# Another order of the query blocks in a differential attention loop on one core

## The chip, the cores and the metric

The kernel runs on one core of one Trainium2 chip, as one program. The metric is the device time of one launch in microseconds (us). Five engines work side by side, each through its own list of instructions in order, and they wait for each other with semaphores: TensorE (PE, matmuls and transposes), VectorE (DVE), ScalarE (ACT), GpSimd (POOL) and SyncE (SP), which starts the transfers.

## What is computed

Two blocks one after the other, on 512 latent tokens of width 1024: two layers with neighbourhood attention, differential attention and a convolution, the first of which also updates 256 context tokens, and then six further sublayers (feed-forward, recurrences, stick-breaking attention). The change lies in the differential attention of layer 0:

```python
def _diff_attend(q1, q2, k1, k2, v, lam):
    '''(softmax(q1 k1^T) - lam * softmax(q2 k2^T)) v, swept over 128-query blocks.'''
    def blk(qs):
        a, b = qs
        s1 = jnp.einsum('bqhd,bkhd->bhqk', a, k1).astype(jnp.float32) * scale
        s2 = jnp.einsum('bqhd,bkhd->bhqk', b, k2).astype(jnp.float32) * scale
        w = jax.nn.softmax(s1, axis=-1) - lam * jax.nn.softmax(s2, axis=-1)
        return jnp.einsum('bhqk,bkhe->bqhe', w.astype(v.dtype), v)
...
b_out = _diff_merge(_diff_attend(rope(q[..., :d]), rope(q[..., d:]), k1, k2, vd, lam), ...)
if update_ctx:      # layer 0 only
    b_c = _diff_merge(_diff_attend(qc[..., :d], qc[..., d:], kc[..., :d], kc[..., d:], vc, lam), ...)
```

There are four heads. The 512 latent queries attend to 768 keys (512 latent and 256 context), the 256 context queries to the 256 context keys alone. The result of each block is normalised over its 96 values and multiplied with a gate.

## The kernel before

Everything runs in fp32 (weights are split into two rounded parts for PE). A stage is a Python object with one method for each engine (`pe`, `act`, `dve`, `pool`) that writes this engine's instructions in order; nothing reorders them afterwards. `LateStage` is the second half of a layer: projections, convolution, and then the differential attention as a loop that is spread over PE, ACT and DVE. POOL has no part in it.

The loop runs over `self.steps` (L1415), a list of pairs (head, query block). In layer 0 `total` is `TA` = 768 tokens, so a head has six blocks of 128 queries: blocks 0 to 3 are latent, 4 and 5 are context. `keys` (L1549) gives 768 keys for blocks 0 to 3, called long or L here, and 256 for 4 and 5, short or S. The list has 24 entries, numbered through as "block 0" to "block 23" below (entry k, whatever its place in the head). In layer 1 `total` is 512, and all 16 entries are long.

What one entry k goes through, with the lines of the profile:

- PE, `scores_pe` (L1601): the scores of both softmaxes, six matmuls of 256 keys (two if short). It waits for the exponentials of entry k-2, whose banks it takes.
- DVE, `max_dve` (L1778): one maximum over both score rows (2 x 768 or 2 x 256).
- ACT, `exp_act` (L1708): two exponentials with sums, waiting for the maximum.
- DVE, `combine_dve` (L1786, L1788, L1791): reciprocals of the sums, and one instruction that joins both into the weights.
- PE, `turn_pe` (L354 by the helper): six transposes, or two if short. It waits for the joined weights, for L1772 of entry k-2 and for ACT's copy of entry k-1; the last four also for L1760 of entry k-1.
- ACT, `copy_act` (L1695, L1699): the transposed weights from PSUM, 256 columns, and 512 more if long.
- PE, `values_pe`: six matmuls with the values, or two.
- DVE, `o_dve` (L1760): scales the output. ACT, `root_act` (L1684, L1686, L1688): its inverse root mean square. DVE, `norm_dve` (L1766): multiplies by it.
- PE, `back_pe`: one transpose back. DVE, `fin_dve` (L1772): multiplies the gate with it.

These steps are skewed by a fixed pattern. In turn k of its loop (L1582) PE does values(k-3), back(k-4), turn(k-2), scores(k+1). ACT (L1672) does root(k-3), copy(k-2), exp(k). DVE (L1743) does:

```python
o_dve(k - 3); fin_dve(k - 4); max_dve(k); combine_dve(k - 1); norm_dve(k - 3)
```

At the end of the loop `drain` puts the begin of the output projection between the last entries: ACT and POOL or DVE split its input pieces (L897, L906), and PE runs three steps of it in each of turns 25 and 26.

PE's matmuls are all recorded on L345 and its transposes on L354, since a helper writes them; an fp32 matmul has two records, a transpose has one.

Of the kernel before, what the change touches and what calls it, by code (L numbers as in the profile page):

```python
# [18 lines left out]
P = 128  # L19
# [4 lines left out]
TA = T + TC  # L24
# [5 lines left out]
DF_HEADS, DF_QK = 4, 48  # L30
# [160 lines left out]
def build(nc, ins, out_dram):  # L191
# [6 lines left out]
    with ctx:  # L198
# [31 lines left out]
        class Area:  # L230
            made = 0

            def __init__(self, start=None):
                self.at = work_at if start is None else start
                self.end = (h_at + 4 * 2 * DT * TA) if start is not None and start < work_at else work_at + 4 * WORK
# [1156 lines left out]
        class LateStage:  # L1392
            def __init__(self, l, total, place, mix, norm, mod):
                self.l, self.total, self.mix, self.tag, self.mod = l, total, mix, f"late{l}", mod
                self.kd, self.qd = place.take(4, TA), place.take(4, TA)
                self.v_at = place.at
                self.v = place.take(6, NA_W)
                self.conv_at = place.at
                self.u = place.take(2, CONV_TOK)
                self.raw = [place.take(T) for _ in range(2)]  # L1400
                self.tmp = [place.take(T) for _ in range(2)]
                self.y = place.take(2, CONV_OUT)
                self.ln_sq = [place.take(T) for _ in range(2)]
                names = lambda g: [(f"w_in{l}", i) for i in IN_PIECE[g]]
                self.conv_of = [Project(names(8), P, norm, total), Project(names(9), P, norm, total)]
                self.k_of = Project(names(2), P, norm, TA)
                self.v_of = ToTokens(Project(names(3), P, norm, TA), self.v, self.raw)
                self.q_of = Project(names(6), P, norm, total)
                self.g_of = Project(names(7), DF_V, norm, total)
                place = Area(h_at)  # L1410
                self.p1, self.p2 = [place.take(TA) for _ in range(2)], [place.take(TA) for _ in range(2)]
                self.pt = [place.take(TA) for _ in range(2)]
                self.o_sb, self.o_sq = [place.take(DF_V) for _ in range(2)], place.take(DF_V)
                self.h_end = place.at
                self.steps = [(h_, i) for h_ in range(DF_HEADS) for i in range(total // P)]  # L1415
                self.n = len(self.steps)
                two = total == TA

                self.taps_at = (10, 6, 4, 2, 4) if two else (10, 6, 4, 4, 2)

                self.ln_at = {"mean": 1, "square": (1, 3), "sum": (2, 4), "root": (2, 4), "silu": 6} if two else {
                    "mean": 0, "square": (0,), "sum": (1,), "root": (1,), "silu": 2}
                self.starts = {0: PAD, T: PAD + T + PAD}
                self.n_y = T if total == T else CONV_OUT
# [2052 lines left out]
```

## Time and profile before

| | |
|---|---|
| time, median of 3 runs | 3408.81 us (3407.46 to 3411.09) |
| the profiled execution | 3408.95 us, of which the span 3407.20 us |
| PE busy in the span | 3203.2 us, 94% |
| DVE, ACT, POOL busy | 1675.6, 1212.0, 715.3 us |
| loop of layer 0, first to last L1760 | 468.64 to 563.30 us from the span's start |
| loop of layer 1, the same | 977.57 to 1045.82 us |

The profile is of one execution. Its times count from the begin of the span. Busy time of PE is modelled at the ends of matmuls, so a PE that reads as busy is not at its peak. A timeline row gives the start, the time taken, the engine, the line, the operation, what it writes and reads, how many instructions are merged in it, and in brackets how long the engine idled before it and which engine and line it had waited for.

### The profile page before, as it was taken

How to read it: one execution, taken by the hardware profiler on the slowest of the kernel's cores; microseconds unless marked ns; L12 is line 12 of the kernel's file. 1: busy time of each engine (PE TensorE's matmuls, PEld its weight loads, DVE VectorE, ACT ScalarE, POOL GpSimd, SP SyncE). 2: the span in 40 equal slices, each digit the busy share in tenths (PEclk: the TensorE clock that was granted, in tenths of full speed). 3: DMA queues.
4: the chain of work that ended last, by engine and by line, in shares of the span. 5: the costliest groups of instructions: out<-in, count | busy, mean ns of one | idle time of the engine just before them, and what ended most of it. 6: DMA issues, size and time to landing. Idle time of an engine off the chain costs nothing.

```text
span 3407.2 us, 40024 instructions
## 1 busy us (share of the span) xinstructions
PE 3203.2 (94%) x16252; PEld 2527.6 (74%) x16252; DVE 1675.6 (49%) x2558; ACT 1212.0 (36%) x2068; POOL 715.3 (21%) x518
## 2 busy tenths in 40 slices
PE   6999988899988999989899999999999999999998
PEld 4777766677866788867788778887888776578886
DVE  2155555415764634457655553446444525564344
ACT  3242165434264322233344332224222325542222
POOL 3204312331513100046332300001000343230000
PEclk9999999999999999999899999999999999999999
DMA  5303210121102233222000133222232231022322
GB/s 225 118 20 115 88 41 24 49 97 47 56 28 78 81 93 105 88 89 93 19 7 1 50 103 108 93 93 87 87 105 87 81 111 38 1 87 93 107 86 80
DMA packets 77575, 260.55 MB, mean 76 GB/s; under 512 B 8400, under 2 KB 9552, under 8 KB 76240
## 3 DMA queue, kind: packets, MB, share of 16 engines
q1 hardware_dynamic: 76528, 253.28, 22.6%
q0 software_dynamic: 864, 4.72, 0.4%
q8 instruction: 129, 2.11, 0.3%
q14 instruction: 54, 0.44, 0.0%
HBM read 255.87 MB, written 2.10 MB: 76 GB/s over the span
## 4 chain that ended last, share of the span: by engine, by line
PE 86%; DVE 7%; ACT 4%; POOL 1%; issue 1%; DMA 1%; SPq 0%; ACTq 0%; DVEq 0%; POOLq 0%
PE banks L345 85%; PE banks L354 1%; POOL w_lo L336 1%; DVE area L576 1%; DVE x_lat L579 1%; DMA area<-in_w_mod 1%; DVE small L1778 0%; DVE area L1722 0%; DVE area L1760 0%; ACT area L434 0%; POOL w_late L336 0%; ACT area L437 0%; ACT w_hi L326 0%; POOL area L410 0%; DVE area L494 0%
## 5 line engine op out<-in xcount | busy, mean ns | idle before, releaser
L345 PE MATMUL banks<-area,w_hi 128*128 128x512 f32 (+4 forms) x5896 | 1770.5, 383 | 24.0 <-POOL w_lo L336 8.1
L345 PEld LDWEIGHTS banks<-area,w_hi 128*128 128x128 f32 (+2 forms) x5896 | 1078.8, 188 | 288.4 <-issue 24.2
L345 PE MATMUL banks<-area,w_lo 128*128 128x512 f32 (+4 forms) x2948 | 1120.2, 381 | 0.0
L345 PEld LDWEIGHTS banks<-area,w_lo 128*128 128x128 f32 (+2 forms) x2948 | 554.8, 188 | 119.1
L345 PE MATMUL banks<-area,w_late 128*128 128x512 f32 (+2 forms) x2316 | 579.1, 399 | 28.8 <-ACT area L532 14.8
L326 ACT ACTIVATE w_hi<-w_raw 128x1024 fp32r<-128x1024 f32 (+2 forms) x361 | 349.5, 971 | 544.9 <-PE banks L345 413.4
L345 PEld LDWEIGHTS banks<-area,w_late 128*128 128x128 f32 (+1 forms) x2316 | 434.6, 190 | 146.3 <-ACT area L532 18.1
L345 PE MATMUL banks<-area,area 128*128 128x64 f32 (+10 forms) x3896 | 468.6, 326 | 71.7 <-DMA area<-in_w_mod 17.5
L345 PEld LDWEIGHTS banks<-area,area 128*128 128x128 f32 (+4 forms) x3896 | 384.0, 183 | 157.7 <-issue 71.9
L410 POOL TENSOR_TENSOR area<-area,area 128x512 f32<-128x512 f32 (+1 forms) x102 | 139.6, 1371 | 1475.2 <-ACT area L395 1473.4
L336 POOL TENSOR_TENSOR w_lo<-w_raw,w_hi 128x1024 fp32r<-128x1024 f32 (+1 forms) x133 | 308.7, 2323 | 455.4 <-ACT w_hi L326 455.4
L336 DVE TENSOR_TENSOR w_lo<-w_raw,w_hi 128x1024 fp32r<-128x1024 f32 (+1 forms) x228 | 263.2, 1155 | 158.7 <-ACT w_hi L326 158.7
L969 ACT ACTIVATE area<-area 128x512 fp32r<-128x512 f32 x88 | 55.6, 632 | 417.7 <-DVE area L1000 417.7
L326 ACT ACTIVATE w_late<-w_raw 128x1024 fp32r<-128x1024 f32 (+2 forms) x103 | 100.9, 979 | 235.9 <-PE banks L345 232.8
L345 PE MATMUL banks<-area,const 128*128 128x512 f32 (+4 forms) x422 | 149.2, 500 | 28.4 <-POOL area L410 8.2
L997 DVE TENSOR_TENSOR area<-banks,area 128x512 f32<-128x512 f32 x80 | 55.2, 691 | 239.1 <-PE banks L345 239.1
L1722 DVE SCALAR_TENSOR_TENSOR area<-area,par,area 128x783 f32<-128x783 f32 (+1 forms) x120 | 149.1, 1302 | 0.0
L862 DVE COPY area<-banks 128x512 f32<-128x512 f32 x72 | 46.9, 661 | 195.4 <-PE banks L345 179.1
L345 PEld LDWEIGHTS banks<-area,const 128*128 128x128 f32 (+3 forms) x422 | 69.4, 193 | 80.5 <-issue 33.7
L336 DVE TENSOR_TENSOR w_late<-w_raw,w_late 128x1024 fp32r<-128x1024 f32 (+1 forms) x76 | 86.1, 1133 | 85.4 <-ACT w_late L326 85.4
L989 DVE TENSOR_TENSOR area<-banks,area 128x512 f32<-128x512 f32 x80 | 55.3, 691 | 105.0 <-PE banks L345 105.0
L354 PE MATMUL banks<-const,area 128*128 128x128 f32 (+1 forms) x438 | 72.3, 284 | 33.9 <-DVE area L1772 21.4
(236 smaller groups left out, 2274.6 us busy)
## 6 DMA issues: line engine op xcount, KB each, us to landing
w_raw<-in_l_ffn_w_in SPq DMA_DIRECT2D x176, 512.0 KB, 3.2
w_raw<-in_l_ffn_w_out SPq DMA_DIRECT2D x128, 384.0 KB, 3.1
w_raw<-in_w_in SPq DMA_DIRECT2D x66, 512.0 KB, 3.5
w_raw<-in_w_mod SPq DMA_DIRECT2D x32, 512.0 KB, 5.4
w_raw<-in_w_qkv SPq DMA_DIRECT2D x24, 512.0 KB, 3.2
w_raw<-in_l_w_in SPq DMA_DIRECT2D x22, 512.0 KB, 3.3
w_raw<-in_w_out SPq DMA_DIRECT2D x32, 320.0 KB, 2.9
area<-in_w_mod SPq DMA_DIRECT2D x8, 1024.0 KB, 16.6
```

The lines of the kernel that those rows point to most:

```text
L326: e.activation(split_bufs(m)[0], raw_of(m), ACT.Copy).then_inc(*sig("w_rounded", "weights hi", m))
L336: e.tensor_tensor(lo, raw_of(m), hi.bitcast(f32), SUB).then_inc(*sig("w_split_dve" if dve else "w_split", "weights", m))
L345: return e.matmul(out, lhsT, rhs, start=first, stop=stop, skip_group_check=True)
L354: return e.transpose(out, in_, ident[0:k, 0:k])
L410: e.tensor_tensor(a, a, self.slot_of(s, j)[:, 0:c1 - c0], ADD).then_inc(*sig("squares_added", *self.tag, "added", s, j))
L576: e.scalar_tensor_tensor(y, y, self.gain(j, s), self.squares.rs[:, c0:c1], MUL, MUL).then_inc(*sig("post_step", self.tag, "step", s, j))
L579: e.tensor_tensor(x, x, y, ADD).then_inc(*sig("x_new", self.tag, "x", s, j))
L862: e.tensor_copy(yy, b).then_inc(*sig("evicted_dve", "evicted", u))
L969: e.activation(self.a_hi[:, j, :], a, ACT.Copy).then_inc(*sig("a_hi", self.tag, "a hi", half, j))
L989: e.tensor_tensor(sg, bank, self.norm.rs, MUL).then_inc(*sig("evicted_dve", "evicted", u))
L997: e.tensor_tensor(a, bank, self.norm.rs, MUL).then_inc(*sig("evicted_dve", "evicted", u))
L1722: e.scalar_tensor_tensor(yy, uu, w, yy, MUL, ADD).then_inc(*sig("taps", self.tag, "tap", m, k))
```

## The change

Within each head of layer 0 the six query blocks are taken in the order 0, 1, 4, 2, 3, 5. The two short blocks, the fourth and fifth index, are apart by two long ones now. Layer 1 keeps its order.

```diff
-                self.steps = [(h_, i) for h_ in range(DF_HEADS) for i in range(total // P)]
+                blocks = (0, 1, 4, 2, 3, 5) if total == TA else range(total // P)
+                self.steps = [(h_, i) for h_ in range(DF_HEADS) for i in blocks]
```

All engines take their order from this list, and buffers go by the entry's number, so waits and buffers stay as they were. The last entry of a head is short in both. Lines below L1415 move down by one.

On PE, in turns 4 to 7 of the loop, the rows before are (`const` is the identity, area_95 and area_96 the joined weights, area_84 and area_85 queries and keys, area_86 the values, area_99 and area_100 the transposed weights, area_101 and area_102 the outputs):

```order
L354 MATMUL banks<-const,area_95 128x128 x6
L345 MATMUL banks<-area_84,area_85 128x256 x2
L345 MATMUL banks<-area_86,area_99 128x96 x6
L354 MATMUL banks<-const,area_102 96x128
L354 MATMUL banks<-const,area_96 128x128 x6
L345 MATMUL banks<-area_84,area_85 128x256 x6
L345 MATMUL banks<-area_86,area_100 128x96 x6
L354 MATMUL banks<-const,area_101 96x128
L354 MATMUL banks<-const,area_95 128x128 x2
L345 MATMUL banks<-area_84,area_85 128x256 x6
L345 MATMUL banks<-area_86,area_99 128x96 x2
```

and now:

```order
L354 MATMUL banks<-const,area_95 128x128 x2
L345 MATMUL banks<-area_84,area_85 128x256 x2
L345 MATMUL banks<-area_86,area_99 128x96 x2
L354 MATMUL banks<-const,area_102 96x128
L354 MATMUL banks<-const,area_96 128x128 x6
L345 MATMUL banks<-area_84,area_85 128x256 x6
L345 MATMUL banks<-area_86,area_100 128x96 x6
L354 MATMUL banks<-const,area_101 96x128
L354 MATMUL banks<-const,area_95 128x128 x6
L345 MATMUL banks<-area_84,area_85 128x256 x6
L345 MATMUL banks<-area_86,area_99 128x96 x6
```

Before, the scores of entry 5 (x2) stand between long transposes and long values, and entry 4 has short transposes and values around long scores. Now entry 2's transposes and values and entry 5's scores are all short and stand together, and everything from entry 3 to entry 4 is long.

On ACT, turn 4 of the loop before (root of entry 1, copies of entry 2, exponentials of entry 4):

```order
L1684 ACTIVATE area_103,small<-area_102 128x96
L1686 ACTIVATE small<-small,const 128x1
L1688 ACTIVATE small<-small 128x1
L1695 ACTIVATE area_99<-banks 128x256
L1699 ACTIVATE area_99<-banks 128x512
L1708 ACTIVATE area_95,small<-banks,small 128x256
L1708 ACTIVATE area_97,small<-banks,small 128x256
```

and now:

```order
L1685 ACTIVATE area_103,small<-area_102 128x96
L1687 ACTIVATE small<-small,const 128x1
L1689 ACTIVATE small<-small 128x1
L1696 ACTIVATE area_99<-banks 128x256
L1709 ACTIVATE area_95,small<-banks,small 128x768
L1709 ACTIVATE area_97,small<-banks,small 128x768
```

The copy of entry 2 lost its second part, and the exponentials of entry 4 are long.

On PE, at the end of the loop, before:

```order
L354 MATMUL banks<-const,area_96 128x128 x6
L345 MATMUL banks<-area_86,area_100 128x96 x6
L354 MATMUL banks<-const,area_101 96x128
L354 MATMUL banks<-const,area_95 128x128 x2
L345 MATMUL banks<-area_86,area_99 128x96 x2
L354 MATMUL banks<-const,area_102 96x128
```

and now:

```order
L354 MATMUL banks<-const,area_96 128x128 x6
L345 MATMUL banks<-area_86,area_100 128x96 x6
L354 MATMUL banks<-const,area_101 96x128
L354 MATMUL banks<-const,area_95 128x128 x6
L345 MATMUL banks<-area_86,area_99 128x96 x6
L354 MATMUL banks<-const,area_102 96x128
```

Entry 22 is now long (x6), where before both last entries were short.

## Rows read from the trace of the kernel before

**Rows 1.** The page, part 1: busy us (share of the span) xinstructions.
```profile
PE 3203.2 (94%) x16252; PEld 2527.6 (74%) x16252; DVE 1675.6 (49%) x2558; ACT 1212.0 (36%) x2068; POOL 715.3 (21%) x518
```

**Rows 2.** Windows: stretch, its length, busy us of each engine, PEclk the granted clock.
```profile
457.70:465.10 7.40, 3.69 (x16) 2.70 (x17) 5.53 (x7) 3.74 (x9) 0.00 (x0) 0.55 0.08 32
465.10:557.40 92.30, 73.88 (x538) 55.77 (x536) 71.89 (x158) 71.61 (x219) 2.72 (x2) 1.00 0.00 1
554.00:557.40 3.40, 1.42 (x8) 0.84 (x7) 3.33 (x8) 3.08 (x8) 2.65 (x2) 1.00 0.00 0
557.40:560.80 3.40, 2.85 (x10) 2.49 (x11) 1.78 (x4) 2.72 (x7) 2.49 (x2) 0.50 0.00 0
```

**Rows 3.** Timeline, DVE, loop of layer 0, L1760: start, us, instruction, [idle before].
```profile
468.64 0.32 DVE L1760 TENSOR_SCALAR area<-banks,small 128x96 f32<-128x96 f32 x1 [1.12 <-PE banks L345]
...
492.99 0.32 DVE L1760 TENSOR_SCALAR area<-banks,small 128x96 f32<-128x96 f32 x1 [0.81 <-PE banks L345]
...
496.92 0.32 DVE L1760 TENSOR_SCALAR area<-banks,small 128x96 f32<-128x96 f32 x1
...
500.91 0.32 DVE L1760 TENSOR_SCALAR area<-banks,small 128x96 f32<-128x96 f32 x1 [1.20 <-PE banks L345]
...
505.51 0.32 DVE L1760 TENSOR_SCALAR area<-banks,small 128x96 f32<-128x96 f32 x1 [2.41 <-PE banks L345]
...
508.79 0.32 DVE L1760 TENSOR_SCALAR area<-banks,small 128x96 f32<-128x96 f32 x1
...
512.67 0.31 DVE L1760 TENSOR_SCALAR area<-banks,small 128x96 f32<-128x96 f32 x1
...
517.55 0.32 DVE L1760 TENSOR_SCALAR area<-banks,small 128x96 f32<-128x96 f32 x1 [0.81 <-PE banks L345]
...
553.94 0.32 DVE L1760 TENSOR_SCALAR area<-banks,small 128x96 f32<-128x96 f32 x1 [1.74 <-PE banks L345]
...
557.24 0.31 DVE L1760 TENSOR_SCALAR area<-banks,small 128x96 f32<-128x96 f32 x1
...
563.30 0.32 DVE L1760 TENSOR_SCALAR area<-banks,small 128x96 f32<-128x96 f32 x1 [3.37 <-PE banks L345]
```

**Rows 4.** Timeline, DVE: an L maximum each in two gaps, L1766 in one.
```profile
493.49 1.74 DVE L1778 TENSOR_REDUCE small<-banks 128x2 f32<-128x1536 f32 x1
...
509.45 1.74 DVE L1778 TENSOR_REDUCE small<-banks 128x2 f32<-128x1536 f32 x1
...
512.49 0.27 DVE L1766 TENSOR_SCALAR area<-area,small 128x96 f32<-128x96 f32 x1
```

**Rows 5.** Timeline, PE: transposes; scores with values; values of an S block; transposes.
```profile
513.66 0.85 PE L354 MATMUL banks<-const,area 128*128 128x128 f32 x6 [0.53 <-DVE area L1772]
...
514.44 3.07 PE L345 MATMUL banks<-area,area 64*128 64x256 f32 x24
...
555.73 0.69 PE L345 MATMUL banks<-area,area 128*128 128x96 f32 x4 [0.66 <-ACT area L1695]
...
557.95 0.66 PE L354 MATMUL banks<-const,area 128*128 128x128 f32 x2 [1.13 <-DVE area L1772]
```

**Rows 6.** Timeline, DVE, the same loop in layer 1 (L blocks only): L1760.
```profile
977.57 0.32 DVE L1760 TENSOR_SCALAR area<-banks,small 128x96 f32<-128x96 f32 x1 [0.68 <-PE banks L345]
...
981.64 0.32 DVE L1760 TENSOR_SCALAR area<-banks,small 128x96 f32<-128x96 f32 x1 [0.53 <-PE banks L345]
...
986.25 0.32 DVE L1760 TENSOR_SCALAR area<-banks,small 128x96 f32<-128x96 f32 x1 [0.81 <-PE banks L345]
```

**Rows 7.** Timeline, ACT, end of the loop: first pieces of the output projection.
```profile
553.00 1.58 ACT L897 ACTIVATE area<-area 128x768 fp32r<-128x768 f32 x2
```

**Rows 8.** Timeline, PE and DVE, begin of the loop: scores; L1791.
```profile
461.41 2.93 PE L345 MATMUL banks<-area,area 64*128 64x256 f32 x12 [5.48 <-ACT area L1708]
...
461.84 1.02 DVE L1791 SCALAR_TENSOR_TENSOR area<-area,small,area 128x768 f32<-128x768 f32 x1
```

## Prediction

> **What bounds the kernel now.** The page comes first. TensorE (PE) is busy 94% of the span [rows 1], so over the whole kernel a stretch costs what keeps PE from running. The change touches one stretch only, the loop over the 24 query blocks of the differential heads of layer 0. The windows view shows what is special there: from 465.10 to 557.40 PE is busy 73.88 of 92.30 us, VectorE (DVE) 71.89 and ScalarE (ACT) 71.61 [rows 2]. No engine is full. The loop is a chain that is handed round between three engines, and what counts is how long one pass lasts. The clearest mark of a pass is the DVE instruction on L1760, which scales a block's output; it can only start when PE has ended the block's value matmuls. I call its starts o(0) to o(23), the distance from one to the next a gap, and gap k the one from o(k-3) to o(k-2). In it PE transposes block k-2, makes the scores of block k+1 and the values of block k-2; DVE takes the maximum of block k and combines block k-1.
>
> With L for a long block (768 keys) and S for a short one (256 keys), one head of before is L L L L S S. The six gaps from o(6) to o(12) are 3.93, 3.99, 4.60, 3.28, 3.88, 4.87, sum 24.56 [rows 3]. What sets each:
> - 4.60: all three PE parts are long (blocks 9, 12, 9). PE sets it: o and the L1772 behind it, six transposes, then scores and values without a break (3.07 in [rows 5]).
> - 3.93 and 3.99: PE has S scores between L transposes and L values. PE idles a little, and the two ACT copies of the transposed block end last.
> - 3.28 and 3.88: S transposes and S values on PE. DVE sets them. In the second it takes an L maximum at 509.45 and an L combine, ends the L1766 at 512.49 + 0.27, and only then starts o at 512.67 [rows 3, 4].
> - 4.87: all L on PE again, but after a gap that DVE set. There L1766 came at the very end, so PE's transpose back, which needs it, comes only behind the next o; L1772 waits for that, the six transposes for L1772 (513.66), and scores and values run from 514.44 for 3.07 [rows 5]. That is 0.27 more than 4.60.
>
> So before has two all-long gaps per head and four in which short PE parts lie beside long ones.
>
> **The change part by part.** It adds and removes no instruction; it reorders heads to L L S L L S. The three PE parts of gap k belong to blocks k-2, k+1, k-2. Those are three apart, and the new order has period three. So all PE parts of a gap now have the same length: two gaps in three are all long, the third is all short. DVE's two parts (blocks k, k-1) are L+S, L+L, S+L in turn, and the L+L falls on the gap in which PE is all short.
>
> - All-short gap (k = 4, 7, ... 22, seven of them). PE needs 0.3 to 0.4 for two transposes (six take 0.85), 0.5 for four score records (24 of scores and values take 3.07) and 0.69 for the values [rows 5], far less than DVE. DVE: in a gap that follows a PE-bound one the L maximum starts 0.50 behind o (492.99, 493.49 [rows 3, 4]); from an L maximum through an L combine and L1766 to the next o takes 512.67 - 509.45 = 3.22 [rows 3, 4]. Sum 3.72. Bounds: 3.71 if DVE's instructions touch, 3.99 if ACT's copies end last as they do in the second gap of before. I take 3.72: ACT's copy of an S block is one instead of two.
> - All-long gap behind it (k = 5, 8, ... 20, six): same neighbours as before's last gap, 4.87. Bounds 4.60 and 4.87. I take 4.87, because L1766 must again come just ahead of o.
> - All-long gap behind a PE-bound one (k = 6, 9, ... 21, six): 4.61. Layer 1, which has L blocks only, shows 986.25 - 981.64 = 4.61 [rows 6], so DVE and ACT can carry even more than they get here.
> - First gap (k = 3): now all L, with no L1772 yet. Layer 1 has the same first gap: 981.64 - 977.57 = 4.07 [rows 6].
> - Gap 23, no scores any more: such a gap ends with ACT's copies and costs 3.93, as the one from 492.99 to 496.92 [rows 3]. Now the transpose back is late, as behind every all-short gap, which adds 4.87 - 4.60: 4.20, bounds 3.93 and 4.20.
> - Gap 24: 557.24 - 553.94 = 3.30 in before [rows 3], for an S block. Now its block is L, which costs 3.93 when ACT is free; ACT isn't quite, it still works on the first two pieces of the output projection (L897, 1.58 from 553.00 on [rows 7]). I take 4.10, bounds 3.93 and 4.61, the price of an all-long gap.
> - Gap 25: 563.30 - 557.24 = 6.06 in before. PE ran three steps of the output projection in it, mostly at the 1.2 GHz level: the clock is 1.00 up to 557.40 and 0.50 up to 560.80 [rows 2]. PE was busy for 2.85 of those 3.40; at 2.4 GHz that work takes half, 1.43 less: 4.63. Before the fall PE was busy only 1.42 of 3.40 [rows 2], because block 22 was short. It is long now, so I expect no fall here: 4.63, bounds 4.63 and 6.06.
>
> Sum from o(0) to o(23): 4.07 + 7 x 3.72 + 6 x 4.87 + 6 x 4.61 + 4.20 + 4.10 + 4.63 = 99.92. Before it is 563.30 - 468.64 = 94.66 [rows 3]. That is 5.26 more.
>
> Ahead of o(0) there is a gain. At 461.41 PE makes the scores of block 2, at half clock, in 2.93, and only then transposes block 0, whose probabilities are ready at 461.84 + 1.02 = 462.86 [rows 8]. With block 2 short the scores take a third, 1.0, and the transposes start at about 463.0, not 464.3. Up to 465.10 PE runs at 0.50 to 0.55 in any case [rows 2], so half of those 1.3 are worth having: 0.65, bounds 0.3 and 1.3.
>
> Behind o(23) nothing is gained back: PE's output projection waits for pieces that need the last block, so it moves as a whole. Total 5.26 - 0.65 = 4.61. The profiled execution took 3408.95 (span 3407.20 and 1.75 around it), 0.14 above the median of 3408.81, so the sum can be put on the median: **3413.4 us**, 0.14% slower. A measurement of this kernel can tell about 0.2%, 6.8 us, from no change, so my forecast is "no difference that counts, on the slow side". If every bound fell to one side the total would be +2.0 (late gaps at 4.61, start gain 1.3, gaps 23 and 24 at 3.93) or +8.8 (all-short gaps at 3.99, start gain 0.3, gap 24 at 4.61, gap 25 at 6.06); as they won't all do so, this case's own range is 3411 to 3417.
>
> **A rule of the skill against a row.** The clock fell at 557.40 although PE had been busy 1.42 of the 3.40 us before, in pieces [rows 2], with no idle time over 1.13 us between them [rows 5]. The Trainium skill (TensorE: Matmul & The Clock Gate, section "Why this matters for your kernels") puts such falls down to a long gap without any matmul, and asks only that bursts have no such gap between them. By that rule the new order would never slow PE's clock in this loop, and the sum stays 4.61. The trace does not agree with it here, and so the first rival gets a real chance.
>
> **Rivals.**
> 1. Slower by more than 0.2%: the clock falls in the all-short gaps. In each, PE has 0.4 + 0.5 + 0.7 of work in 3.72, then one transpose back, then waits again for L1772: from the middle of the gap to the middle of the late transposes it is busy about as little as it was from 554.00 to 557.40 [rows 2]. For: that row. Against: an all-long gap lies on either side, and in before, where two S blocks follow each other, the clock stayed 1.00 for all 92.30 us [rows 2]. Price: a stretch like 557.40 to 560.80 [rows 2] at half clock, laid on an all-long gap, costs half of what PE works in it, 1.4 by that row, at most 1.7. There are seven such gaps. It decides from two falls on: 4.61 + 2 x 1.4 = 7.4. With two or three falls I get 3416 to 3418; middle 3417.
> 2. Not slower, 3408.8: engines have the same total work per head, and queues absorb the order. Before's 18.4 us of idle PE leave room in principle. Against: o waits for the values and DVE runs in order, so there is no slack to average over; nor is there any behind the loop.
> 3. Faster, 3404.9: the all-short gap closes at PE's pace of about 2.5 instead of DVE's 3.72, seven times 1.2 less than in the sum, 8.5 in all, so 4.61 - 8.5 = -3.9. It would need o to start ahead of the L maximum and L combine that stand before it on DVE. [rows 4] speak against it.
>
> **How the numbers follow.** Forecast 0.54, rival 1 0.32, rival 2 0.10, rival 3 0.04. The forecast's own range, 3411 to 3417, passes +6.8 in about one case in ten, rival 1 in nearly nine of ten: slower 0.33. Faster comes from rival 3 and a sliver of noise: 0.05. The rest, 0.62, is within 0.2%. The range runs from 3410 to 3419: it leaves out rivals 2 and 3 below and a clock that falls four times or more above, under 2 in 10 together.
>
> **What would show it.** In the profile after, the starts of the output scaling should come at gaps of 4.87, 4.61, 3.72 in turn, 13.20 per three blocks (26.4 a head against 24.56); in the 3.72 gap DVE should never idle and PE should; o(0) about 0.65 earlier; granted clock 1.00 through the loop and at its end. I am wrong if the clock row dips inside the loop (rival 1), if the all-short gap is far from 3.72, or if an all-long gap is not PE's.

## Result and profile after

| | before | after |
|---|---|---|
| time, median of 4 runs | 3408.14 us (3407.10 to 3411.09) | 3435.32 us (3433.07 to 3436.57) |
| the profiled execution, its span | 3408.95, 3407.2 us | 3436.07, 3434.3 us |
| first to last output scaling, layer 0 | 94.66 us | 118.68 us |
| first to last output scaling, layer 1 | 68.25 us | 71.04 us |

After takes 1.0076 times as long, with a 95% interval of 1.0061 to 1.0091: 27 us slower, where 4.6 were forecast, and far outside the range of 3410 to 3419. The span grew by 27.1 us. Of that 24.02 lie in the loop of layer 0, -0.94 ahead of it (467.70 against 468.64 for the first scaling), 2.79 in the loop of layer 1, whose code is the same, and about 1.2 elsewhere.

Page part 1 of after; columns as in [rows 1]:
```profile
PE 3226.1 (94%) x16252; PEld 2543.0 (74%) x16252; DVE 1674.6 (49%) x2558; ACT 1213.1 (35%) x2068; POOL 715.8 (21%) x518
```

VectorE, ScalarE and GpSimd do the work of before in the same time [rows 1]. PE has 22.9 us more of busy time for the same 16252 instructions, so its instructions became longer.

Timeline of after, DVE, L1761, the output scaling. The columns are start, us, instruction and idle before it, as in [rows 3]; one line is added to the file, so L1760 is L1761 now:
```profile
475.49 0.31 DVE L1761 TENSOR_SCALAR area<-banks,small 128x96 f32<-128x96 f32 x1
...
483.10 0.32 DVE L1761 TENSOR_SCALAR area<-banks,small 128x96 f32<-128x96 f32 x1 [4.48 <-PE banks L345]
...
487.70 0.32 DVE L1761 TENSOR_SCALAR area<-banks,small 128x96 f32<-128x96 f32 x1 [1.34 <-PE banks L345]
...
491.42 0.31 DVE L1761 TENSOR_SCALAR area<-banks,small 128x96 f32<-128x96 f32 x1
...
497.90 0.32 DVE L1761 TENSOR_SCALAR area<-banks,small 128x96 f32<-128x96 f32 x1 [3.48 <-PE banks L345]
...
567.66 0.31 DVE L1761 TENSOR_SCALAR area<-banks,small 128x96 f32<-128x96 f32 x1
...
573.95 0.32 DVE L1761 TENSOR_SCALAR area<-banks,small 128x96 f32<-128x96 f32 x1 [3.16 <-PE banks L345]
...
579.84 0.32 DVE L1761 TENSOR_SCALAR area<-banks,small 128x96 f32<-128x96 f32 x1 [3.43 <-PE banks L345]
...
586.38 0.32 DVE L1761 TENSOR_SCALAR area<-banks,small 128x96 f32<-128x96 f32 x1 [4.09 <-PE banks L345]
```

The gap up to 487.70 is 4.60, the one up to 491.42 is 3.72: both as forecast. But the gaps from 475.49 to 483.10 and from 491.42 to 497.90 are 7.61 and 6.48, where the prediction has 4.87, and DVE idles 4.48 and 3.48 in them, waiting for PE. These two values alternate through the loop, three times each. The last three gaps are 6.29, 5.89 and 6.54.

Windows of after; columns as in [rows 2], the third number from the end is the granted clock:
```profile
471.90:475.30 3.40, 1.66 (x10) 1.02 (x10) 3.33 (x6) 2.45 (x8) 0.00 (x0) 1.00 0.00 0
475.30:482.10 6.80, 5.94 (x25) 4.35 (x25) 2.93 (x9) 3.30 (x12) 0.00 (x0) 0.50 0.00 0
482.10:492.40 10.30, 7.00 (x51) 5.21 (x51) 7.63 (x17) 7.24 (x22) 0.00 (x0) 1.00 0.01 2
492.40:495.80 3.40, 3.40 (x16) 2.73 (x18) 1.95 (x5) 2.16 (x8) 0.00 (x0) 0.50 0.00 0
495.80:506.00 10.20, 7.78 (x60) 5.80 (x56) 6.62 (x13) 6.08 (x18) 0.00 (x0) 1.00 0.00 0
567.50:584.50 17.00, 13.53 (x52) 11.22 (x53) 7.00 (x20) 10.77 (x29) 5.45 (x3) 0.50 0.00 0
```

Between 471.90 and 506.00 the clock is 0.50, the 1.2 GHz level, in 475.30:482.10 and 492.40:495.80, and 1.00 outside them. The pattern goes on with 506.0 to 512.8, 523.1 to 526.5, 536.7 to 543.5 and 553.8 to 557.2, and a last stretch of 17.0 us at 0.50 lies over the end of the loop. That is one fall for each of the seven all-short gaps; it comes at the gap's end, and the gap behind pays for it. The low stretch is 6.8 us long where that gap takes 7.61, and 3.4 us where it takes 6.48. Before had 1.00 for 92.30 us [rows 2].

Timeline of after, PE, around the first fall:
```profile
472.49 0.41 PE L354 MATMUL banks<-const,area 128*128 128x128 f32 x2 [0.65 <-DVE area L1773]
472.83 1.32 PE L345 MATMUL banks<-area,area 64*128 64x256 f32 x8
475.63 0.45 PE L354 MATMUL banks<-const,area 128*96 128x128 f32 x1 [1.48 <-DVE area L1767]
476.61 1.51 PE L354 MATMUL banks<-const,area 128*128 128x128 f32 x6 [0.53 <-DVE area L1773]
478.05 5.01 PE L345 MATMUL banks<-area,area 64*128 64x256 f32 x24
```

In the all-short gap PE does short transposes (472.49), short scores and values (472.83), and then idles 1.48 us until L1767 lets it make the transpose back. From there on all is slow: six transposes take 1.51 and scores with values 5.01, where [rows 5] have 0.85 and 3.07. The transpose back takes 0.45 instead of the 0.31 of before's at 508.83, where the clock is 1.00. Together 0.66 + 1.94 + 0.14 = 2.74, and that is 7.61 - 4.87.

### The profile page after: what moved, and what is told of

It is laid out like the page before. It is cut to its first block, busy times and chain, and to the rows that moved or that the text cites. A ratio compares the mean times of both kernels' runs of the same rounds, so it can differ in the third digit from the quotient of the medians.

```text
span 3434.3 us, 40024 instructions
## 1 busy us (share of the span) xinstructions
PE 3226.1 (94%) x16252; PEld 2543.0 (74%) x16252; DVE 1674.6 (49%) x2558; ACT 1213.1 (35%) x2068; POOL 715.8 (21%) x518
## 4 chain that ended last, share of the span: by engine, by line
PE 87%; DVE 6%; ACT 3%; POOL 1%; issue 1%; DMA 1%; SPq 0%; ACTq 0%; DVEq 0%; POOLq 0%
PE banks L345 85%; PE banks L354 2%; POOL w_lo L336 1%; DMA area<-in_w_mod 1%; DVE small L1779 0%; DVE area L576 0%; DVE x_lat L579 0%; DVE area L1723 0%; ACT area L434 0%; DVE area L1761 0%; DVE area L1773 0%; POOL w_late L336 0%; ACT area L437 0%; ACT w_hi L326 0%; POOL area L410 0%
## 5 line engine op out<-in xcount | busy, mean ns | idle before, releaser
L345 PE MATMUL banks<-area,area 128*128 128x64 f32 (+10 forms) x3896 | 482.1, 334 | 68.3 <-DMA area<-in_w_mod 16.0
L345 PEld LDWEIGHTS banks<-area,area 128*128 128x128 f32 (+4 forms) x3896 | 393.0, 188 | 159.4 <-issue 74.2
L354 PE MATMUL banks<-const,area 128*128 128x128 f32 (+1 forms) x438 | 80.1, 307 | 41.8 <-DVE area L1773 21.0
```

The source lines that it names most:

```text
L345: return e.matmul(out, lhsT, rhs, start=first, stop=stop, skip_group_check=True)
L354: return e.transpose(out, in_, ident[0:k, 0:k])
```

## Experiments

Kernels that are compared share runs of the kernel before on the same chip, and their ratios are to those. Times in us. "Loop" is the first to the last output scaling of layer 0.

| kernel | median | ratio, 95% interval | loop | all-short gaps with a fall behind them |
|---|---|---|---|---|
| before, runs beside the first four | 3407.19 | | | |
| e1_filled | 3417.41 | 1.0028 (1.0017 to 1.0038) | 102.88 | 0 of 7 |
| e2_uneven | 3413.12 | 1.0015 (1.0006 to 1.0024) | 95.72 | has none |
| e3_three_heads | 3426.01 | 1.0055 (1.0041 to 1.0069) | 111.56 | 5 of 5 |
| e4_before_filled | 3405.14 | 0.9996 (0.9987 to 1.0005) | 93.43 | has none |
| before, runs beside the next four | 3407.81 | | | |
| e5_all_filled | 3411.94 | 1.0012 (1.0003 to 1.0021) | 100.18 | 0 of 7 |
| e6_one_each | 3423.98 | 1.0045 (1.0031 to 1.0058) | 107.78 | 2 of 7 |
| e7_borders_filled | 3406.08 | 0.9988 (0.9979 to 0.9997) | 93.41 | has none |
| e8_after_again | 3433.71 | 1.0069 (1.0055 to 1.0083) | 119.58 | 7 of 7 |
| e9_head_0, one execution | 3409.21 | before beside it 3409.68 | 98.82 | 1 of 1 |
| e10_head_1, one execution | 3411.77 | before beside it 3409.68 | 101.14 | 2 of 2 |

### e1_filled: the same order, PE kept busy in the all-short gaps

Three fp32 matmuls of two constants (128x256) that nobody reads stand behind the values of each short block but the last, which is in seven places. They write the unused half of a PSUM bank.

```diff
+                self.fills = {(k, "values"): 3 for k in range(5, 24, 3)} if total == TA else {}
...
                     if 3 <= k < self.n + 3:
                         self.values_pe(q, e, k - 3)
+                        self.fill_pe(q, e, k, "values")
...
+            def fill_pe(self, q, e, k, place):
...
+                for _ in range(self.fills.get((k, place), 0)):
+                    mm(e, banks[6 if k < 2 else 2 if k >= 24 else 7][:, 256:512], ones, C("cos")[:, 0:256], True, True)
```

> The changed kernel with three more matmuls (128x128 times 128x256, fp32, into the unused half of PSUM bank 7, result never read) behind the values of each short block, where PE waits for DVE anyway; seven times. Theory clock: the new order alone costs what the instruction chain says (gaps 4.87, 4.61, 3.72), and the rest of the +27 us comes from PE's clock falling to 1.2 GHz in the all-short gaps. Then the granted clock stays 1.00 from 466 us to the end of the loop, gaps are 4.87, 4.61, 3.72, and the time is 4 to 6 us above before, about 3413. Theory chain: the new order makes the gaps long by itself (waits between the engines) and the low clock is only a sign of an idle PE. Then more work on PE gains nothing or costs its own time, 7 x 1.3 = 9 us: 3435 to 3444.

The timeline of DVE for e1 (L1772 is the output scaling) and two windows:
```profile
475.20 0.31 DVE L1772 TENSOR_SCALAR area<-banks,small 128x96 f32<-128x96 f32 x1
...
480.07 0.32 DVE L1772 TENSOR_SCALAR area<-banks,small 128x96 f32<-128x96 f32 x1 [1.88 <-PE banks L345]
```
```profile
465.10:557.40 92.30, 78.09 (x546) 59.13 (x544) 66.83 (x146) 65.22 (x202) 0.00 (x0) 0.99 0.00 1
561.80:568.60 6.80, 6.26 (x25) 5.33 (x25) 1.87 (x5) 3.45 (x9) 3.62 (x2) 0.51 0.00 0
```

The gap behind the all-short one is 4.87, six times out of six, and the mean clock over 92.30 us is 0.99, low only at its begin. The order is that of after, and the added work, if it did anything but hold the clock, could only cost. So what made 7.61 and 6.48 out of 4.87 is the clock, which fell with PE's own work alone in the gap and held with three matmuls more, and nothing in the chain of waits. The loop is 15.80 shorter than in after.

The time is 10.2 us above before, where 4 to 6 were expected, and the clock did not hold to the end of the loop as expected: from 561.8 it is at half, and gaps 24 and 25 took 4.83 and 6.88, together 2.7 more than in e5 below, where it holds. Another 2.8 lie in layer 1's loop (71.03 us), which the change does not touch (see e8).

### e2_uneven: short blocks apart, but not three apart

```diff
-                self.steps = [(h_, i) for h_ in range(DF_HEADS) for i in range(total // P)]
+                self.steps = [(h_, i) for h_ in range(DF_HEADS)
+                              for i in ((0, 1, 2, 4, 3, 5) if total == TA else range(total // P))]
```

> Only the order of before changed, to blocks 0, 1, 2, 4, 3, 5: the two short blocks are apart too, but by two and four places instead of three. So the scores of a short block (three places ahead of its transposes and values) never meet short transposes and values. Theory distance three: no gap is all short on PE, the clock stays 1.00 in the loop, and by hand the gaps of a head come to 4.61, 3.72, 4.20, 4.61, 3.93, 3.35 = 24.4 against 24.56: 3407 to 3410. Theory separation: what costs is that short blocks no longer follow each other; then this order loses most of the 27 us too, 3425 or more.

```profile
465.10:557.40 92.30, 73.84 (x535) 56.30 (x535) 72.70 (x157) 72.20 (x219) 2.74 (x2) 0.98 0.00 1
554.00:557.40 3.40, 1.92 (x11) 1.71 (x9) 2.53 (x4) 2.91 (x7) 1.91 (x2) 0.61 0.01 2
```

The short blocks don't follow each other here either, and no gap within the loop sees the clock fall. The first low stretch is at the loop's end, from 554.7 on, a gap earlier than in before: it comes behind gap 23 (2.65 us), in which PE has a short block's transposes and values and no scores. The loop is 1.06 longer than before's. So taking the short blocks apart is not what costs most. What costs is that they stand three apart, since PE's three parts of a gap belong to blocks three apart.

The time missed its expectation: 3413.12, which is 5.9 above before and clear of it, where 3407 to 3410 was expected. The loop gives 1.06 of this and layer 1's loop 2.8 (71.02 us). The eleven runs lie between 3404.88 and 3418.19, and the eight longest have a lower mean clock (0.975 to 0.977) than the other three (0.979, 0.980). Only one of the other three has a profile, so where the clock fell in the eight is open. It is far from the 3425 of the rival.

### e3_three_heads: the new order in heads 0 to 2

```diff
+                              for i in ((0, 1, 4, 2, 3, 5) if total == TA and h_ in (0, 1, 2) else range(total // P))]
```

> The changed kernel with the old order in head 3 alone. Five all-short gaps are left (gaps 4, 7, 10, 13, 16 of the loop) and the end of the loop is as in before. Theory clock: three heads cost 1.9 each by the chain less 0.65 at the begin, and five falls at 1.6 to 2.7 each, 10.7: about +15 over before, 3423; the clock is low once behind each of these five and not for 17 us on end at the loop's end. Theory even: the cost is spread over the heads alike, three quarters of 27: +20, 3428.

```profile
535.70:542.50 6.80, 5.92 (x24) 4.33 (x25) 2.96 (x9) 3.32 (x12) 0.00 (x0) 0.50 0.00 0
542.50:573.50 31.00, 23.12 (x168) 17.75 (x167) 23.34 (x52) 24.64 (x74) 4.21 (x2) 1.00 0.00 1
573.50:576.90 3.40, 3.40 (x13) 2.97 (x12) 1.04 (x2) 1.42 (x2) 2.08 (x2) 0.53 0.00 0
```

Five all-short gaps, five falls, behind them 7.63, 6.49, 7.61, 6.48 and 7.60. In head 3, with the old order, the clock is 1.00 for 31 us up to the fall at the loop's end that before has as well. The time is 18.8 us above before and lies between the two expectations, 15 and 20, so it does not decide; the clock and the gaps do. The five falls cost 11.5 and the rest of the loop 5.4 more than before's, both near what the theory of the clock has; layer 1's loop, again 71.03, adds 2.8.

### e4_before_filled: the kernel before with PE kept busy at both ends of the loop

```diff
+                self.fills = {(0, "scores"): 10, (24, "back"): 1, (24, "turn"): 1, (25, "back"): 2} if total == TA else {}
```

> The kernel before with more matmuls of the same unused kind where PE idles around this loop: ten behind the scores of block 1 (PE waits 5.5 us there) and four in turns 24 and 25. Theory clock: PE runs at 1.00 instead of 0.50 from 461 to 465 and from 557 to 561: 1.4 us less at the end, 1 to 1.8 us less at the begin, 3405 to 3406, unless the matmuls themselves delay the work behind them. Rival: what PE waits for at these two places does not depend on the clock, and the time stays 3408.

```profile
457.70:465.10 7.40, 6.24 (x48) 4.56 (x46) 6.15 (x10) 6.18 (x15) 0.00 (x0) 1.00 0.00 1
554.00:557.40 3.40, 3.35 (x20) 2.95 (x20) 1.38 (x2) 2.33 (x6) 2.76 (x2) 1.00 0.00 0
```

Before has 0.55 in the first stretch [rows 2]; here it is 1.00, and the first scaling comes at 464.71 instead of 468.64. Of these 3.93 the clock gives 1.80: from the scores of block 2 to the first scaling it is 5.43 us (459.28 to 464.71) instead of 7.23 (461.41 to 468.64). The other 2.13 passed before those scores, in stages ahead of the loop. At the end gap 25 takes 4.81 instead of 6.06. The last scaling is 5.16 earlier than in before's trace, but the medians differ by 2.05 only, with an interval that holds 1: single traces of one kernel differ by some us in what lies outside this loop.

### e5_all_filled: the order of after, no low clock anywhere in the loop

```diff
+                self.fills = {**{(k, "values"): 3 for k in range(5, 24, 3)}, (0, "scores"): 10, (23, "turn"): 1, (24, "back"): 1, (24, "turn"): 2, (25, "back"): 1} if total == TA else {}
```

> The changed kernel with the seven groups of unused matmuls behind the values of short blocks (three each), ten behind the scores of block 1, and five in turns 23 to 25 at the end of the loop, where PE waits in pieces. Theory clock: now nothing is left of the low clock around this loop. PE is at 1.00 from 457 us to the end of the loop; gaps 4.07, then 3.72, 4.87, 4.61 in turn, about 4.2, 4.1 and 4.6 at the end, 99.9 to 100.5 in all. Against the kernel before with the same filling (loop 93.4) the order alone costs 6.5 to 7, less 0.4 that a short third block saves at the begin: 3410 to 3413. If the first filled kernel's 4.83 and 6.88 at the end have another cause than the clock, these two stay: 3 us more.

Timeline of PE, with the fill of the first all-short gap, and windows:
```profile
471.63 1.32 PE L345 MATMUL banks<-area,area 64*128 64x256 f32 x8
472.78 1.49 PE L345 MATMUL banks<-const 128*128 128x256 f32 x6
...
475.27 0.85 PE L354 MATMUL banks<-const,area 128*128 128x128 f32 x6 [0.53 <-DVE area L1785]
476.05 3.08 PE L345 MATMUL banks<-area,area 64*128 64x256 f32 x24
```
```profile
465.10:557.40 92.30, 78.53 (x554) 59.58 (x554) 66.83 (x146) 66.13 (x204) 0.00 (x0) 1.00 0.00 1
558.00:575.00 17.00, 15.66 (x92) 12.96 (x92) 8.56 (x17) 9.86 (x24) 8.87 (x5) 1.00 0.01 1
```

The fills (1.49, six records for three fp32 matmuls) lie in PE's pause and delay nothing; transposes take 0.85 and scores with values 3.08 again. The clock is 1.00 up to 575. Now the loop is 100.18, where the prediction's chain has 99.92, and the kernel is 4.13 us slower than before (1.0 to 7.2 by the interval), where the prediction has 4.61. Against e4's loop, the old order with the clock held, the new one costs 6.75, as expected. But of the 0.4 that a short third block was to save at the begin there is nothing: from the scores of block 2 to the first scaling it is 5.43 us in both, since PE now waits 0.81 for DVE's weights there. Gaps 24 and 25, 4.83 and 6.88 in e1, are 4.23 and 4.79: they too had been the clock. Beside e8, which is after run on the same chip, it is 21.8 us faster in the medians, and in the profiles the loop is 19.40 shorter.

### e6_one_each: one fill in each all-short gap in place of three

```diff
+                self.fills = {(k, "values"): 1 for k in range(5, 24, 3)} if total == TA else {}
```

> The changed kernel with only one unused matmul (0.4 us) behind the values of each short block instead of three. If the clock falls because PE does little in these gaps, one may do for some of them: fewer than seven falls, the time between 3417 and 3435, each fall 1.6 to 2.8 us. If only the idle piece of 1.5 us counts, which one matmul cuts to 1.0, all seven should be gone: 3417.

```profile
465.10:516.80 51.70, 40.77 (x294) 30.32 (x293) 36.40 (x80) 36.62 (x115) 0.00 (x0) 0.99 0.00 1
516.80:520.20 3.40, 3.40 (x16) 2.71 (x18) 1.83 (x5) 2.08 (x7) 0.00 (x0) 0.51 0.00 0
520.20:558.00 37.80, 29.26 (x212) 21.56 (x209) 26.89 (x59) 26.09 (x80) 0.00 (x0) 1.00 0.00 1
558.00:575.00 17.00, 14.36 (x55) 12.15 (x56) 5.96 (x16) 9.59 (x24) 5.44 (x3) 0.50 0.00 0
```

One fill, half a us of work, keeps the clock in all of these gaps but one (gap 14 is 6.51) and the last, behind which the clock stays low to the end of the loop, as in after. The seven gaps are alike in PE's instructions; behind two of them the clock fell and behind five it did not. The longest idle time of PE is alike too, 1.01 or 1.02 in each, where after has 1.48. So the length of the idle piece alone does not decide it: then all seven should have held, or none. What holds the clock in one gap need not hold it in the next of the same form, and why is open.

### e7_borders_filled: e4, and matmuls in four pauses of PE elsewhere

In before's trace PE also waits at the begin of the feed-forward stages and finds the clock low behind the wait. Eight unread matmuls stand ahead of each of these stages.

```diff
+                for _ in range(8):
+                    mm(e, banks[7][:, 256:512], ones, C("cos")[:, 0:256], True, True)
                 for half, (project, out) in enumerate(self.halves):
                     project.pe(q, e, lead=0 if half else self.LEAD)
```

> The kernel before with the filling at the begin and end of this loop, and eight unused matmuls (3.5 us) at the begin of each of the four feed-forward stages, where PE idles 3.71 us for the norm. Theory clock: the fall behind each of these four pauses goes too, worth 1.5 to 3 us each since PE has work without a break behind them; with the 5 us of the loop 10 to 15 less than before: 3392 to 3398. Rival: behind the pauses the stage waits for weights, not for PE's clock; then 3403 to 3405.

Timeline of PE behind the first of these pauses, first of before, then of e7:
```profile
1101.48 0.79 PE L345 MATMUL banks<-area,w_hi 128*128 128x512 f32 x1 [3.71 <-ACT area L532]
1102.07 0.63 PE L345 MATMUL banks<-area,w_lo 128*128 128x512 f32 x1
```
```profile
1097.44 0.50 PE L345 MATMUL banks<-area,w_hi 128*128 128x512 f32 x1 [0.26 <-ACT area L532]
1097.77 0.39 PE L345 MATMUL banks<-area,w_lo 128*128 128x512 f32 x1
...
1099.87 0.73 PE L345 MATMUL banks<-area,w_hi 128*128 128x512 f32 x2 [0.31 <-DVE area L538]
```

One matmul takes 0.39 instead of 0.63, the clock is held. But at once PE waits for DVE (0.31 at 1099.87): the producer of its input sets the pace there. So little is won, and the expected 3392 to 3398 is missed: 3406.08, 1.7 us under the runs of before, interval 0.9979 to 0.9997. Against e4's 0.9996 (0.9987 to 1.0005) the intervals overlap, so that the four pauses are worth anything is not shown.

### e8_after_again: after, a second time

> The changed kernel once more, unchanged. Whether the clock falls depends on when a pause of PE falls, and that may differ from run to run. If the falls were chance, another execution shows fewer than seven in the loop, and times that scatter from 3413 up; if the order itself keeps them in step, seven again, with gaps behind the short one of 7.6 and 6.5 in turn, and 3433 to 3437.

Timeline of DVE, L1761:
```profile
475.09 0.31 DVE L1761 TENSOR_SCALAR area<-banks,small 128x96 f32<-128x96 f32 x1
...
481.60 0.32 DVE L1761 TENSOR_SCALAR area<-banks,small 128x96 f32<-128x96 f32 x1 [3.51 <-PE banks L345]
...
489.92 0.31 DVE L1761 TENSOR_SCALAR area<-banks,small 128x96 f32<-128x96 f32 x1
...
497.70 0.32 DVE L1761 TENSOR_SCALAR area<-banks,small 128x96 f32<-128x96 f32 x1 [4.72 <-PE banks L345]
```

Seven falls again and a loop of 119.58, but now the first one costs 6.51 - 4.87 = 1.64 and the second 7.78 - 4.87 = 2.91: the alternation is there and has changed places. The end of layer 1's loop took 4.57 and 5.01, as in before (4.57, 4.99); in after's profile it was 5.52 and 6.83. In after's the clock was 0.50 from 1062.4 to 1069.2, in the two others it was 1.00 there. The long form (70.9 to 71.0 us for this loop) is also in the profiles of e2, e7 and e10, and the short one in that of e5: it goes with no order of layer 0. So these 2.8 us are no effect of the change, but of whether the clock fell there in that execution. One of the four times, 3427.51, is below the 3433 to 3437 expected.

### e9_head_0 and e10_head_1: one and two all-short gaps

By now the falls could still be a matter of repetition: five or seven such pauses, one every 15 to 16 us. Two kernels use the new order in one head only, the first in head 0 (`h_ in (0,)`), which gives one all-short gap, and the second in head 1, which gives two.

> The new order in head 0 alone, so the loop has one all-short gap, gap 4 (blocks 2 and 5), and all else is as before. Theory, one such gap is enough whatever went before it: gap 4 is 3.72, the clock is 0.50 behind its middle, and gap 5 takes 6.5 to 7.6 instead of 4.87; first to last output scaling 94.66 plus about 0.6 for the chain plus 1.6 to 2.8 for the fall, near 97 to 98. Rival, the order has to repeat the pause every head or half head before the clock gives way: gap 5 is 4.87 and no stretch between the first and the last output scaling reads below 1.00 except the one at the end of the loop that the kernel before has too; loop near 95.3.

```profile
471.60:475.00 3.40, 1.68 (x11) 1.02 (x10) 3.33 (x6) 2.37 (x8) 0.00 (x0) 1.00 0.00 0
475.00:481.80 6.80, 5.87 (x24) 4.28 (x25) 3.00 (x9) 3.37 (x12) 0.00 (x0) 0.50 0.00 0
481.80:556.70 74.90, 60.51 (x447) 46.19 (x447) 57.83 (x126) 57.41 (x176) 0.00 (x0) 1.00 0.00 1
```

> The new order in head 1 alone, so the loop has two all-short gaps, gap 7 (blocks 5 and 8) and gap 10 (blocks 8 and 11), with head 0 in the old order in front of them. Theory, each such gap lowers the clock by itself: gaps 8 and 11 take 6.5 and 7.6 or the reverse instead of 4.87, clock 0.50 in both and 1.00 elsewhere in the loop up to its end; loop near 94.66 + 1.2 + 4.4 = 100. Rival, repetition: gaps 8 and 11 are 4.87, or only the second is longer; loop 96 to 98.

```profile
467.20:487.80 20.60, 15.30 (x109) 11.08 (x108) 16.13 (x37) 15.47 (x52) 0.00 (x0) 1.00 0.00 1
487.80:491.20 3.40, 3.40 (x16) 2.69 (x17) 1.79 (x5) 2.04 (x7) 0.00 (x0) 0.50 0.00 0
491.20:501.50 10.30, 7.66 (x58) 5.67 (x54) 6.85 (x15) 6.31 (x18) 0.00 (x0) 1.00 0.00 0
501.50:508.30 6.80, 6.14 (x26) 4.55 (x26) 2.73 (x8) 3.10 (x12) 0.00 (x0) 0.50 0.00 0
```

A single all-short gap is enough: gap 5 of e9 takes 7.58, and then the clock is 1.00 for 74.90 us. In e10 gaps 8 and 11 take 6.51 and 7.67, and head 0 ahead of them is as in before. Repetition is ruled out, as far as one profile of each can do so. Each fall belongs to its own pause. Their loops are 98.82 and 101.14, each about 1 over what was expected (97 to 98, near 100). The times of these two, one execution each, can't be compared with a single run of before beside them; the gaps can.

## Why the prediction was wrong

Point by point. The last columns are the gaps in after and in e5, where the clock is 1.00:

| step | predicted | after | e5 |
|---|---|---|---|
| first gap | 4.07 | 4.07 | 4.07 |
| all-short gap, seven | 3.72 | 3.71 or 3.72 | 3.71 or 3.72 |
| all-long behind it, six | 4.87 | 7.61, 6.48 in turn | 4.87 or 4.88 |
| all-long behind a PE-bound one, six | 4.61 | 4.60 or 4.61 | 4.61 |
| gap 23 | 4.20 | 6.29 | 4.20 |
| gap 24 | 4.10 | 5.89 | 4.23 |
| gap 25 | 4.63 | 6.54 | 4.79 |
| loop | 99.92 | 118.68 | 100.18 |

- **The chain of waits: right.** Every gap came out within 0.01 in after or in e5, but for gaps 24 and 25, for which the forecast was 0.13 and 0.16 too low. That DVE sets the all-short gap and PE the others, and that the transpose back comes late behind a gap that DVE set, is confirmed. In e5 the loop is 5.52 longer than before's, where 5.26 were forecast. That its time is 4.13 above before, so near to 4.61, is in part luck: its filled begin runs at full clock, and its first scaling is 2.14 earlier than before's, where the forecast has 0.65.
- **The begin: not settled.** 0.65 was forecast; after's first scaling is 0.94 earlier than before's. But of two others with the old begin e2 has it at 468.68 and e10 at 467.19, and five others with the new begin and no fills there lie between 466.64 and 468.33. The scatter is as large as the gain. In e4 and e5, where the clock is 1.00 there, the short third block gained nothing (5.43 us in both).
- **"Granted clock 1.00 through the loop and at its end": wrong**, and this is the step that failed. The clock fell at each of the seven all-short gaps, in after and in e8, and PE's work in the gaps behind them took up to 1.8 times as long. Rival 1 named the mechanism and the place. Its chance was too low and its size far too small, in three ways. It allowed two or three falls where all seven gaps had one. It priced one at 1.4, at most 1.7, as a stretch of 3.40 at half clock; that is right for three of the six (1.61), but in the others the clock stayed low for 6.8 us, over all the transposes, scores and values, and they cost 2.74. And it had no price for a fall at the end of the loop, where one low stretch lies over gaps 23 to 25 and costs 18.72 - 13.22 = 5.50 against e5. Together 3 x 2.74 + 3 x 1.61 + 5.50 = 18.6 of the 18.76 us by which the loop missed the forecast. The whole miss is 22.6 in the medians; 2.8 more of it are layer 1's loop in after's profile, and no part of the change.
- **Gap 25: wrong twice.** The prediction let the fall of before vanish, since block 22 became long. But in gap 22 all PE parts are short, and the clock fell there, three gaps earlier, and stayed low. And halving PE's work to get 4.63 took off a little too much: with the clock held it is 4.79 in e5, and in before's order 4.81 (e4).
- **The row that was misread.** The prediction held against rival 1 that in before the clock stayed at 1.00 where two short blocks follow each other. This window of before shows what PE does there:

```profile
508.80:512.20 3.40, 2.83 (x19) 1.92 (x19) 3.26 (x6) 2.86 (x10) 0.00 (x0) 1.00 0.00 0
```

It is busy 2.83 of 3.40 us, since the scores in that gap are those of a long block. In after PE is busy 1.66 of 3.40 (471.90:475.30 above). The one row of before that resembled this was 554.00:557.40 with 1.42 [rows 2], and right behind it the clock fell. The nearest row should have weighed most, for each of the seven gaps alike. There was no reason in the rows for "two or three".

The prediction was right to set a row against the rule of the Trainium skill (TensorE: Matmul & The Clock Gate, section "Why this matters for your kernels"): the trace of after has no idle time of PE over 1.48 us in any all-short gap, and the clock fell all the same. Yet the conclusion drawn from that, a chance of 0.32, was half-hearted. Rivals 2 and 3 didn't occur.

What is faster than either kernel is the order of before with PE kept busy in its pauses (e7, 0.12% under before). It is little. In the one pause shown above PE waits for DVE at once where the clock is held; whether the others are alike is not shown.

## What to carry to other kernels

Before reordering a pipelined loop, write down for each pass how much work each engine gets. A period of the order that equals the distance between the stages puts all small pieces of an engine into one pass, and all large ones into another; the first waits for another engine, and on PE it may also lose the clock, for which the next pass pays. Where such a pass can't be avoided, a few matmuls that nobody reads, put into the pause, delayed nothing here (the gap stays 3.71) and were worth 22 us (e5 against e8). And where one row shows a bad effect under the conditions that the change will create, price it at every place with these conditions, not at some.

## What the runs showed of the hardware

- The clock fell without a long pause. PE was busy 1.66 of 3.40 us, the longest idle time was 1.48 us, and behind it the clock was 0.50. The Trainium skill (TensorE: Matmul & The Clock Gate, section "Why this matters for your kernels") names long gaps without a matmul as the cause. The longest idle time of PE in this loop is 1.48 us, so by that rule nothing would have happened; the trace does not agree.
- One such pause is enough, with a gap full of PE's work on either side (e9). Between a fall and the next the clock came back to 1.00 each time, except at the end of the loop, where PE had pauses of its own and it stayed at 0.50 for 17 us.
- The cost of a fall took two values, 1.6 and 2.7 to 2.9 us, in the same code. The two alternated within one execution, and which came first differed between executions (after and e8). The cheaper goes with 3.4 us at the low level, the dearer with 6.8. What decides between them is open.
- With one fill per gap, the clock held in five of seven gaps of the same instructions; with three it held in all.
